# Gating a selective scan inside the scan: sigmoid from exponentials and reciprocals, moved beside the next block's work

## The reference, cut to what matters

```python
y = y_diag + y_off + d_skip.reshape(SSD_GROUPS, SSD_HPG, 1) * xs
y = y.reshape(b, L, SSD_WIDTH).astype(z.dtype)
yg = (y * jax.nn.silu(z)).reshape(b, L, SSD_GROUPS, SSD_WIDTH // SSD_GROUPS)
yg = rms_norm(yg, norm_g.reshape(SSD_GROUPS, -1))
```

## Time and profile before

| | |
|---|---|
| time, median of 3 runs | 1654.37 us (1654.34 to 1654.7) |
| the profiled execution: its own time | 1655.09 us |
| its span in the trace | 1653.0 us (2.1 us lie around it) |
| TensorE's granted clock, mean | 0.989 of full |
| PE / DVE / ACT / POOL busy, share of the span | 96% / 68% / 37% / 65% |

### The profile page before, as it was taken

One profiled execution on the slowest core, in us unless ns is written; L12 is line 12 of the kernel. 1 busy time (PEld: TensorE's weight loads), 2 busy tenths in 40 slices (PEclk: granted clock), 3 DMA queues, 4 the chain that ended last, 5 costly groups with the idle time before them and its releaser, 6 DMA issues.

```text
span 1653.0 us, 25961 instructions
## 1 busy us (share of the span) xinstructions
PE 1594.9 (96%) x9085; PEld 1444.8 (87%) x9085; DVE 1127.8 (68%) x2412; ACT 619.0 (37%) x909; POOL 1074.9 (65%) x550
## 2 busy tenths in 40 slices
PE   7999878999899999999999999989999999999998
PEld 6799847977799999999999999968888888888888
DVE  6772475300679999738999996266777676767766
ACT  3133465210233333345555555333333232333331
POOL 5453301644269888767666665668788989888863
PEclk9999979999999999999999999999999999999999
DMA  5222113231269888869999998999999999999961
GB/s 202 77 77 77 39 51 119 102 113 40 88 200 310 301 301 300 278 219 329 335 345 337 353 333 292 325 363 346 363 351 342 353 365 360 358 362 351 365 238 45
DMA packets 172517, 417.78 MB, mean 253 GB/s; under 512 B 13088, under 2 KB 97696, under 8 KB 167328
## 3 DMA queue, kind: packets, MB, share of 16 engines
q1 hardware_dynamic: 133856, 257.52, 43.9%
q0 software_dynamic: 36864, 134.23, 23.9%
q10 hardware_dynamic: 1728, 25.17, 3.8%
HBM read 360.25 MB, written 56.62 MB: 252 GB/s over the span
## 4 chain that ended last, share of the span: by engine, by line
PE 68%; DMA 3%; issue 1%; DVE 1%; POOL 0%; SPq 0%; ACT 0%; DVEq 0%; POOLq 0%
PE s_psum L1295 32%; PE s_psum L1345 27%; PE s_psum L1329 5%; DMA scores<-gate_scratch 2%; PE s_psum L199 1%; PE s_psum L200 1%; PE s_psum L201 1%; DMA s_gtile<-in_v_t,s_v_row 1%; POOL s_gtile L1281 0%; DVE s_lo L1681 0%; DVE s_psum L1675 0%; DMA s_raw<-in_u_t 0%; PE s_psum L212 0%; SPq L1183 0%; SPq L1217 0%
## 5 line engine op out<-in xcount | busy, mean ns | idle before, releaser
L1247 POOL TENSOR_TENSOR s_lo<-s_raw,s_hi 128x1024 fp32r<-128x1024 f32 x224 | 538.8, 2406 | 242.7 <-ACT s_hi L1401 239.8
L1295 PE MATMUL s_psum<-hn_hi,s_hi 128*128 128x384 f32 x1024 | 347.7, 340 | 6.5 <-ACT s_hi L1401 6.5
L1295 PE MATMUL s_psum<-hn_lo,s_hi 128*128 128x384 f32 x1024 | 343.4, 335 | 0.0
L1401 ACT CAST s_hi<-s_raw 128x1024 fp32r<-128x1024 f32 x256 | 266.3, 1046 | 174.7 <-PE s_psum L1345 69.8
L1345 PE MATMUL s_psum<-s_hi,s_whi 128*128 128x512 f32 x768 | 299.1, 391 | 6.1 <-DVE s_lo L1681 4.4
L1345 PE MATMUL s_psum<-s_hi,s_wlo 128*128 128x512 f32 x768 | 298.1, 389 | 0.0
L1345 PE MATMUL s_psum<-s_lo,s_whi 128*128 128x512 f32 x768 | 298.0, 389 | 0.0
L1281 POOL DMA_INDIRECT s_gtile<-in_v_t,s_v_row x128 | 210.5, 1645 | 25.0 <-issue 24.1
L1295 PEld LDWEIGHTS s_psum<-hn_hi,s_hi 128*128 128x128 f32 x1024 | 193.5, 189 | 6.7 <-ACT s_hi L1401 6.7
L1295 PE MATMUL s_psum<-hn_hi,s_lo 128*128 128x384 f32 x1024 | 198.0, 334 | 0.0
L1295 PEld LDWEIGHTS s_psum<-hn_lo,s_hi 128*128 128x128 f32 x1024 | 193.5, 189 | 0.0
(11 more groups left out here) (290 smaller groups left out, 2795.5 us busy)
## 6 DMA issues: line engine op xcount, KB each, us to landing
s_raw<-in_u_t SPq DMA_DIRECT2D x128, 512.0 KB
s_raw<-in_v_t SPq DMA_DIRECT2D x128, 512.0 KB
act_scratch<-s_acts SPq DMA_DIRECT2D x128, 192.0 KB
gate_scratch<-s_gtile ACTq DMA_DIRECT2D x12, 2048.0 KB, 9.0
scores<-act_scratch SPq DMA_DIRECT2D x32, 768.0 KB
scores<-gate_scratch SPq DMA_DIRECT2D x32, 768.0 KB
m_w_raw<-in_w_in SPq DMA_DIRECT2D x11, 1024.0 KB, 4.8
m_w_raw<-in_w_q SPq DMA_DIRECT2D x8, 1024.0 KB, 4.8
```

The costliest lines, as they stand in the source:

```text
L1247: pool.tensor_tensor(lo[:, s, :], raw[:, s, :], hi[:, s, :].bitcast(F32), ALU.subtract).then_inc(lo_ready[s], 1)
L1295: return pe.matmul(psU[:, s % 2, :], uu[:, s, d * P:(d + 1) * P], hh[:, d, P:T], start=start, stop=stop)
L1401: act.copy(hi[:, s, :], raw[:, s, :]).then_inc(hi_ready[s], 1)
```

## The change

- ACT: after each z half arrives, `zexp(t)` gets exp(-z) (Exp straight from PSUM, 256 columns), ahead of the copy to `zs`. `zexp(t)` is half of `ropeA` or `ropeB`, by t's parity, so from t = 2 on it waits for `scan_gated`. The four Silu activations behind the loop go.
- DVE: `gate_scan(t)` becomes: `zexp` + 1; `ym` times `zs`; reciprocal of `zexp` (512 elements a partition); `ym` times that; the two sums of squares as before. It is called for block t-1 within the scan's step t, between L899 and L904, and for the last block at attention step i = 0, between `find_maxima(0)` and `find_maxima(1)`.
- `SSD_ROOT_AT` goes from 6 to 3: the root on ACT at step 3, the reciprocal and `finish_scan` on DVE at steps 4 to 7.
- `layer_input` 0 to 3 move from PE's steps 2 to 5 to steps 4 to 7 (`E_AT = 4`), with ACT's share and the banks' order.

```diff
-SSD_ROOT_AT = 6
-PIN_AT = (2, 3)
+SSD_ROOT_AT = 3
+PIN_AT, E_AT = (2, 3), 4
...
-        elif i < PC + TB:
-            out += [(("e", i - PC), "e_ready", 2 * (i - PC) + 2)]
+        elif E_AT <= i < E_AT + TB:
+            out += [(("e", i - E_AT), "e_ready", 2 * (i - E_AT) + 2)]
...
+        zexp = lambda t: (ropeA, ropeB)[t % 2][:, 1, :]
...
-                    me.did(act.copy(zs[:, t, half * 256:(half + 1) * 256], src), sem["z_copied"])
+                    cs = slice(half * 256, (half + 1) * 256)
+                    if t >= 2:
+                        act.wait_ge(sem["scan_gated"], t - 1)
+                    me.did(act.activation(zexp(t)[:, cs], src, ACT.Exp, scale=-1.0), sem["z_ready"])
+                    me.did(act.copy(zs[:, t, cs], src), sem["z_copied"])
...
-            act.wait_ge(sem["z_copied"], 2 * TB)
-            for t in range(TB):
-                me.did(act.activation(zs[:, t, :], zs[:, t, :], ACT.Silu), sem["z_ready"])
...
+            def gate_scan(t):
+
+                ym = mix[:, t, 0:SSD_W]
+                dve.wait_ge(sem["z_ready"], 2 * t + 2)
+                dve.wait_ge(sem["z_copied"], 2 * t + 2)
+                me.did(dve.tensor_scalar(zexp(t), zexp(t), 1.0, None, ALU.add))
+                step(dve.tensor_tensor(ym, ym, zs[:, t, :], ALU.mult))
+                step(dve.reciprocal(zexp(t), zexp(t)))
+                step(dve.tensor_tensor(ym, ym, zexp(t), ALU.mult), sem["scan_gated"])
+                for g in range(SSD_G):
+                    yg = ym[:, g * 256:(g + 1) * 256]
+                    me.did(dve.tensor_tensor_reduce(ropeB[:, 0, g * 256:(g + 1) * 256], yg, yg, 1.0, 0.0, ALU.mult, ALU.add, col(ssq, 2 * t + g)),
+                           sem["ssd_sums"] if g else None)
+                me.settle()
+
...
+                if t:
+                    gate_scan(t - 1)
...
-            def gate_scan(t):
-
-                ym = mix[:, t, 0:SSD_W]
-                dve.wait_ge(sem["z_ready"], t + 1)
-                step(dve.tensor_tensor(ym, ym, zs[:, t, :], ALU.mult))
...
-                if 1 <= i <= TB:
-                    gate_scan(i - 1)
+                if i == 0:
+                    gate_scan(TB - 1)
```

More of the change, by code:

```diff
@@ L320, in mixer_and_retrieval @@
                  "k_loaded", "gain_loaded", "h_stored", "row_ready", "con_loaded", "cols_loaded", "p_loaded", "pThi_ready", "pT_ready", "e_ready", "e_stored",
-                 "scan_ready", "eps_set", "ssd_sums", "ssd_root", "early_sums", "early_root", "e_sums", "e_root"]
+                 "scan_ready", "scan_gated", "eps_set", "ssd_sums", "ssd_root", "early_sums", "early_root", "e_sums", "e_root"]
         sem = {n: new_sem("m_" + n) for n in names}
@@ L600, in _ @@
                     tile_done(last)
-                elif i < PC + TB:
-                    layer_input(i - PC)
+                elif E_AT <= i < E_AT + TB:
+                    layer_input(i - E_AT)
             for j in range(TB, 2 * TB):
@@ L752, in _ @@
                     me.did(act.copy(pT_hi[:, j, :], bank.filled(act, "pT", j)), sem["pThi_ready"])
-                elif PC <= j < PC + TB:
-                    take_layer_input(j - PC)
+                elif E_AT <= j < E_AT + TB:
+                    take_layer_input(j - E_AT)
             act.wait_ge(sem["fin_sums"], 1)
```

## The result

| | before | after |
|---|---|---|
| time, median of 10 runs | 1654.36 us (1652.1 to 1660.18) | 1658.18 us (1655.58 to 1661.3) |
| the profiled execution: its own time, its span | 1655.09, 1653.0 us | 1658.24, 1656.5 us |

The ratio is 1.0021, with a 95% interval of 1.0012 to 1.0029: 3.8 us slower, where the prediction had 3.6. PE is busy 96% of the span as before; the cost lies where the edit is.

The account below looks back on a forecast made before the run. PE is busy 96%, but in scan and attention DVE's order was taken to decide: +8.7 us at unit 0, +14.8 at unit 1, falling to +3.6 at unit 11; 1655.1 + 3.6 = 1658.7, 1658.0 as median; range 1649.5 to 1662.

Parts of the forecast that it names:

- The lock in block 3: End of the scan: one DVE instruction with two SBUF inputs gets in per POOL instruction; unit 0 starts 8.7 us later.
- the reciprocal's length: In each gate on DVE: 3.35 us for 512 elements, from 6.25 ns an element, in a gate of 6.1 us.
- Without the lock: Rival, block 3: the gate's instructions get in ahead of POOL; end 8.4 us earlier, 1649.6 us; chance 0.17.
- a short reciprocal: Rival, the gates: reciprocal takes 0.69 us, last gate 3.45; end 2.7 us earlier, 1655.3 us; chance 0.10.
- The walk: Attention, DVE's starts of units: +14.8 us at unit 1, +5.0 at unit 4, +3.6 at unit 11.
- PE isn't late: Scan, blocks 1 and 2: PE's `y` of block 3 has some 2 us to spare, so PE loses nothing.
- the overrun of the two gates: Scan, blocks 1 and 2: gate 1.1 us too long for DVE's wait; state and next decays late by 1.2.
- units 6 and 8: Attention: unit 6 starts at 233.2 us, 7.7 later than before; unit 8 at 239.4, 5.4 later.
- the width given to the moved layer inputs: Rival, units 4 to 8: if ACT, not PE, binds, up to 2 us either way; within the main case, 0.50.
- From unit 11 on both do the same: From attention unit 11 to the end: both kernels run alike, so unit 11's 3.6 us shift reaches the end.
- The high end of 4.4 us for the reciprocal: In each gate: reciprocal at 8 ns an element, +1.0 us in the last gate; among the worse cases, chance 0.18.

Follow-up runs that it names:

- e1_short_recip: The changed kernel with the reciprocal over 64 of the 512 columns, the rest of the denominator not inverted; 1655.39 us, ratio to the kernel before 1.0009.
- e2_new_gate_late_cut: The changed kernel with POOL's cut of the output projection's first weight tile held until the attention's outputs are scaled; 1655.21 us, ratio to the kernel before 1.0008.

## Why the prediction was right, and where it wasn't

- **The mechanism and its price are shown.** The lock in block 3 and the reciprocal's length were the two terms that carried the sum. Without the lock the changed kernel takes 8.0 us less, with a short reciprocal 2.8 less (8.4 and 2.7 were forecast for these rivals). The second match is luck: 2.7 was the last gate alone, and in the traces the short reciprocal gives 4.1 net by unit 1, the 2.8 of the last gate and 1.3 at the scan's end.
- **That 3.6 and 3.8 agree so well is luck too.** The ratio's interval allows 2.0 to 4.8 us, and the two traces have 3.9 at unit 11 and 3.0 at part 2.
- **The walk held nearly row by row.** Net starts of units 0, 1, 2, 4, 6, 8, 11 are 212.1, 218.75, 220.2, 224.8, 233.8, 240.1, 248.1; forecast were 211.95, 218.8, 220.2, 225.0, 233.2, 239.4, 247.8.
- **The step that failed: "PE isn't late"** in blocks 1 and 2. I looked at `y` of block 3, which had 2 us to spare, and not at the bank that the late adds of block 1 free. It cost PE 1.0 us (e1_short_recip takes it away). DVE's own list lost 1.0 more by the second gate, which is too long for its wait as well: the prediction had counted the overrun of the two gates once, 1.2, where it is 2.0, so DVE reached block 3's gate at net 195.4 instead of 194.6. That hardly mattered, as POOL's cuts set the end of block 3. They began 1.1 late with PE, at net 194.3, where the prediction had them begin in place and be pushed back 0.7 by DVE's turns; pushed back they were not, as they took 13.5 us in all against 13.6 before. So one mistake covers the other, and the second product ends at net 208.3; 208.2 was forecast.
- **Mis-sized: units 6 and 8**, by 0.6 and 0.7 us, inside the width given to the moved layer inputs; unit 4 is 0.2 early. Unit 11 is 3.9 late, not 3.6.
- **"From unit 11 on both do the same" was 0.9 off.** Part 2 begins net 3.0 later. Between units 11 and 15 DVE of before waits 0.72 and 0.29 us for PE's scores, and in after it has no such wait. The rows of the stretch, before and then after, give a granted clock of 0.83 and 1.00:

```profile
243.00:253.00 10.00, 8.29 (x41) 4.84 (x40) 8.55 (x33) 6.15 (x17) 0.00 (x0) 0.83 0.01 2
```
```profile
243.00:253.00 10.00, 7.96 (x49) 4.80 (x47) 9.18 (x36) 8.44 (x28) 0.00 (x0) 1.00 0.13 54
```

  The medians are nevertheless 3.8 apart; one profiled execution of each can't settle a microsecond.
- **A split that I had not made.** The prediction did not price the root's move and the layer inputs' by themselves. They are worth 6 us together and cover most of what the gate costs, and they are not the new gate's merit: before takes them as well (with the root at 5, behind its last gate), and gains 5 us.
- **A slip without effect.** The high end of 4.4 us for the reciprocal is 4.2 by its own 8 ns an element (353 ns + 480 x 8 ns).

## What to carry to other kernels

Before moving work into another engine's idle time, look at what runs beside it: instructions with two SBUF inputs cost 0.69 us in one block and 5.01 in the next, by what POOL did meanwhile. And look up every bank and buffer that the delayed instructions free, not only the value that they make. When a change bundles a costly edit with cheap reorderings, time the reorderings alone on the old kernel, and together: here they were the gain, and the edit was the loss.

## What the runs add on the hardware

- A tensor_scalar of 512 fp32 from SBUF to SBUF on DVE, single source, waits for POOL as well, which the walk had assumed without a row: 1.10 and 2.04 us instead of 0.42. The reciprocal, single source too, does not: 3.35 beside POOL and without it.
- Reciprocal of 64 elements a partition 0.55 us, of 512 3.35: 6.25 ns an element, so the slope of the earlier trace rows held up to 16 times their length. By the Trainium skill, page "VectorE: DVE Perf Modes", section "First, the fixed hardware budget", its repeat count is 8; read as 8 cycles an element at the page's 0.96 GHz that would be some 4.3 us, an estimate. The measured 3.35 decides.
- POOL pays little for the lock: its four cuts took 13.5 us with DVE's gate in between them and 13.6 before, with L904 and L909 in between. In e2_new_gate_late_cut four such cuts took 13.1 (269.94 to 283.04), with no DVE instruction of two SBUF inputs beside them.
